# The last three rows of a final RMSNorm, shared out anew between ScalarE, GpSimd and VectorE

## The reference, cut to what matters

```
y = y @ w_out                    # layer 1, the pooling mixer
x = x + gate[:, None, :] * y
return rmsnorm(x, final_g)       # y = x * rsqrt(mean(x*x) + EPS); y * g
```

## Time and profile before

| | |
|---|---|
| median of 3 runs | 1291.89 us (1291.62 to 1292.37) |
| span of the profiled execution | 1290.2 us |
| TensorE busy in it | 1266.2 us, 98% |
| VectorE busy | 985.9 us, 76% |
| ScalarE busy | 642.3 us, 50% |
| GpSimd busy | 315.3 us, 24% |

### The profile page before, as it was taken

How to read it: one execution, slowest core, us unless ns; L and a number is a source line. 1 busy time by engine, 2 the same in 40 slices (tenths; PEclk the granted TensorE clock), 3 DMA queues, 4 the chain that set the end, 5 groups by cost and what they waited for, 6 DMA issues and landing times.

```text
span 1290.2 us, 15455 instructions
## 1 busy us (share of the span) xinstructions
PE 1266.2 (98%) x5639; PEld 1044.3 (81%) x5639; DVE 985.9 (76%) x1155; ACT 642.3 (50%) x904; POOL 315.3 (24%) x182
## 2 busy tenths in 40 slices
PE   5999999999999999999999999999999999999997
PEld 5877888888888888888888888888888888888886
DVE  6889987878878886868467599848748747797677
ACT  7466656465646464635558465234233333443353
POOL 0033443433424343000000013132223121413200
PEclk8999999999999999999999999999999999999999
DMA  9812232323242332597847302232232232882053
GB/s 289 224 49 70 80 121 81 107 83 114 62 122 70 115 106 75 169 382 269 310 155 270 113 17 66 68 97 65 69 95 66 66 98 76 292 285 66 18 177 132
DMA packets 151507, 167.31 MB, mean 130 GB/s; under 512 B 6342, under 2 KB 125318, under 8 KB 151432
## 3 DMA queue, kind: packets, MB, share of 16 engines
q1 hardware_dynamic: 151432, 166.33, 40.0%
HBM read 141.14 MB, written 25.17 MB: 129 GB/s over the span
## 4 chain that ended last, share of the span: by engine, by line
PE 90%; DVE 6%; SPq 1%; issue 1%; ACT 0%; DMA 0%; DVEq 0%; ACTq 0%
PE psum L2382 30%; PE psum L2384 29%; PE psum L2383 29%; DVE whole_x L1985 1%; DVE w_lo L1532 1%; DVE X L1622 1%; SPq L626 1%; PE psum L2529 1%; PE psum L2586 0%; SPq L615 0%; DMA whole_x<-in_mod_w 0%; DVE bufs L1767 0%; DVE w_lo L1554 0%; DVE late L1615 0%; SPq L618 0%
## 5 line engine op out<-in xcount | busy, mean ns | idle before, releaser
L2382 PE MATMUL psum<-X,w_hi 128*128 128x512 f32 x1252 | 489.9, 391 | 1.1 <-DVE X L1666 0.8
L2384 PE MATMUL psum<-X,w_lo 128*128 128x512 f32 x1252 | 488.0, 390 | 0.0
L2383 PE MATMUL psum<-X,w_hi 128*128 128x512 f32 x1252 | 487.9, 390 | 0.0
L2382 PEld LDWEIGHTS psum<-X,w_hi 128*128 128x128 f32 x1252 | 235.5, 188 | 52.2 <-issue 1.7
L2384 PEld LDWEIGHTS psum<-X,w_lo 128*128 128x128 f32 x1252 | 235.4, 188 | 49.4
L2383 PEld LDWEIGHTS psum<-X,w_hi 128*128 128x128 f32 x1252 | 235.5, 188 | 48.6 <-issue 0.2
L984 ACT ACTIVATE w_hi<-ssum 128x512 fp32r<-128x512 f32 x156 | 97.1, 626 | 143.2 <-PE psum L2384 106.8
L1532 DVE TENSOR_TENSOR w_lo<-raw,w_hi 128x1024 fp32r<-128x1024 f32 x82 | 100.9, 1230 | 79.2 <-ACT w_hi L962 78.8
L1554 DVE TENSOR_TENSOR w_lo<-ssum,w_hi 128x512 fp32r<-128x512 f32 x156 | 131.2, 849 | 25.6 <-ACT w_hi L984 25.0
L913 POOL TENSOR_TENSOR ssum<-raw 128x512 f32<-128x512 f32 x39 | 72.8, 1868 | 312.4 <-DMA raw<-in_pool_w_in 253.2
L921 POOL TENSOR_TENSOR ssum<-ssum,raw 128x512 f32<-128x512 f32 x39 | 61.3, 1572 | 340.4 <-DVE w_lo L1554 340.4
(11 more groups left out here) (275 smaller groups left out, 1989.7 us busy)
## 6 DMA issues: line engine op xcount, KB each, us to landing
raw<-in_hy_w_in SPq DMA_DIRECT2D x48, 512.0 KB, 5.1
raw<-in_hy_w_out SPq DMA_DIRECT2D x48, 512.0 KB, 5.1
raw<-in_pool_w_in SPq DMA_DIRECT2D x32, 512.0 KB, 5.0
aux<-in_mod_w SPq DMA_DIRECT2D x16, 512.0 KB, 3.9
y_dram<-bufs SPq DMA_DIRECT2D x16, 512.0 KB, 2.7
raw<-in_mod_w SPq DMA_DIRECT2D x16, 512.0 KB, 5.9
y_dram<-gb_ SPq DMA_DIRECT2D x16, 512.0 KB, 3.4
raw<-in_pool_w_out SPq DMA_DIRECT2D x16, 512.0 KB, 5.9
```

What stands on the lines that cost most here:

```text
L2382: nc.tensor.matmul(out_, whi, xhi, start=first, stop=False, skip_group_check=check)
L2383: nc.tensor.matmul(out_, whi, xlo, start=False, stop=False, skip_group_check=check)
L2384: return nc.tensor.matmul(out_, wlo, xhi, start=False, stop=last, skip_group_check=check)
```

## The change

Rows 5 and 6 are no longer scaled and weighted by one VectorE instruction each. ScalarE scales each of them (`scaled_row`), GpSimd weights row 5 and the first half of row 6 in place, VectorE weights the second half of row 6. For row 7 VectorE multiplies each half by `final` into `PARTS[0]` as soon as its residual is there, and after the reciprocal VectorE scales the first half and ScalarE the second. The reciprocals of rows 5 and 6 move ahead in VectorE's order, and the two halves of row 7's residual are separated. The stores wait for the new semaphores.

```diff
@@ -514,6 +514,10 @@
         out_in = [sem(f"out_in{kp}") for kp in range(KP)]
         out_hi = sem("out_hi")
         out_lo = sem("out_lo")
+        row_scaled = sem("row_scaled")
+        last_final = sem("last_final")
+        half_row = sem("half_row")
+        last_scaled = sem("last_scaled")
         pair_part = sem("pair_part")
         pair_added = sem("pair_added")
 
@@ -741,7 +745,13 @@
                     sp.dma_start(bias1, row).then_inc(bias_in, 16)
 
             def store(b):
-                sp.wait_ge(row_ready, b + 1)
+                if b < 5:
+                    sp.wait_ge(row_ready, b + 1)
+                elif b == 5:
+                    sp.wait_ge(half_row, 1)
+                else:
+                    sp.wait_ge(half_row, 2)
+                    sp.wait_ge(row_ready, 6)
                 sp.dma_start(out[0, b * P:(b + 1) * P, :], XN[1][b]).then_inc(out_done, 16)
 
 
@@ -881,7 +891,10 @@
             for b in range(4, SB - 1):
                 store(b)
             for half, cols in enumerate(HALVES):
-                sp.wait_ge(row_ready, SB + half)
+                if half == 0:
+                    sp.wait_ge(row_ready, 7)
+                else:
+                    sp.wait_ge(last_scaled, 1)
                 sp.dma_start(out[0, (SB - 1) * P:SB * P, cols], XN[1][SB - 1][:, cols]).then_inc(out_done, 16)
             sp.wait_ge(out_done, 16 * (SB + 1))
 
@@ -950,6 +963,12 @@
                                         blocks[:, XOPS["B12"], 1, :], ALU.subtract).then_inc(t13_added, 1)
             for q in range(OUT, len(PAIRS)):
                 sums_of_weights(q)
+
+            pool.wait_ge(gate_in, 32)
+            pool.wait_ge(row_scaled, 1)
+            nc.gpsimd.tensor_tensor(XN[1][5], XN[1][5], final, ALU.mult).then_inc(half_row, 1)
+            pool.wait_ge(row_scaled, 2)
+            nc.gpsimd.tensor_tensor(XN[1][6][:, S1], XN[1][6][:, S1], final[:, S1], ALU.mult).then_inc(half_row, 1)
 
         @block.scalar
         def _(act):
@@ -1499,8 +1518,16 @@
                     step_splits(step)
                 if n in (2, 3, 4, 5):
                     squares(1, n - 2)
-            for b in range(4, SB - 1):
-                squares(1, b)
+            def scaled_row(b):
+
+                act.wait_ge(rstd_ready, SB + b + 1)
+                nc.scalar.activation(XN[1][b], XR[1][b], ACT.Copy, scale=rstd[:, 2, b:b + 1]).then_inc(row_scaled, 1)
+
+            squares(1, 4)
+            squares(1, 5)
+            scaled_row(5)
+            squares(1, 6)
+            scaled_row(6)
 
             b = SB - 1
             for half, cols in enumerate(HALVES):
@@ -1515,6 +1542,10 @@
                 else:
                     nc.scalar.activation(sd[:, 2, b:b + 1], ss[:, 2, b:b + 1], ACT.Sqrt, scale=1.0 / D,
                                          bias=ss[:, 1, b:b + 1]).then_inc(root_done, 1)
+            act.wait_ge(rstd_ready, 2 * SB)
+            act.wait_ge(last_final, 2)
+            nc.scalar.activation(XN[1][b][:, S2], PARTS[0][:, S2], ACT.Copy, scale=rstd[:, 2, b:b + 1])\
+              .then_inc(last_scaled, 1)
 
         @block.vector
         def _(dve):
@@ -2000,14 +2031,24 @@
                 nc.vector.scalar_tensor_tensor(out=XN[1][b], in0=XR[1][b], scalar=rstd[:, 2, b:b + 1], in1=final,
                                                op0=ALU.mult, op1=ALU.mult).then_inc(row_ready, 1)
 
+            def times_final(half):
+
+                b, cols = SB - 1, HALVES[half]
+                dve.wait_ge(o_evac, o_count(1, b, half))
+                nc.vector.tensor_tensor(PARTS[0][:, cols], XR[1][b][:, cols], final[:, cols], ALU.mult)\
+                  .then_inc(last_final, 1)
+
+            def second_half_of_row_6():
+                dve.wait_ge(row_scaled, 2)
+                nc.vector.tensor_tensor(XN[1][6][:, S2], XN[1][6][:, S2], final[:, S2], ALU.mult).then_inc(row_ready, 1)
+
             def last_row_out():
                 b = SB - 1
                 inverse(1, b)
                 dve.wait_ge(rstd_ready, 2 * SB)
-                for cols in HALVES:
-                    nc.vector.scalar_tensor_tensor(out=XN[1][b][:, cols], in0=XR[1][b][:, cols],
-                                                   scalar=rstd[:, 2, b:b + 1], in1=final[:, cols],
-                                                   op0=ALU.mult, op1=ALU.mult).then_inc(row_ready, 1)
+                dve.wait_ge(last_final, 1)
+                nc.vector.tensor_scalar(XN[1][b][:, S1], PARTS[0][:, S1], rstd[:, 2, b:b + 1], None, ALU.mult)\
+                  .then_inc(row_ready, 1)
 
             def modulation_1():
                 dve.wait_ge(*full("mod1"))
@@ -2369,10 +2410,14 @@
             residual(1, 4)
             residual(1, 5)
             row_out(4)
+            inverse(1, 5)
             residual(1, 6)
-            row_out(5)
-            residual(1, 7)
-            row_out(6)
+            residual(1, 7, (0,))
+            inverse(1, 6)
+            times_final(0)
+            residual(1, 7, (1,))
+            times_final(1)
+            second_half_of_row_6()
             last_row_out()
 
         @block.tensor
```

## The result

The changed kernel is slower by 0.21%: its runs have a median of 1295.43 us (21 runs), those of the kernel before, taken with them, 1292.56 us (21 runs); the ratio is 1.0021, 95% interval 1.0015 to 1.0027. Applied to the 1291.89 us from which the prediction started, that is 1294.60 us where 1294.4 was forecast. Of the 1.03 us between 1294.4 and the median of 1295.43, 0.67 is that the kernel before itself came out at 1292.56 in these runs. The same changed kernel, run again later, gave 1.0014, interval 1.0005 to 1.0023 (10 runs).

The account below looks back on a forecast made before the run. TensorE bounds most of the span, then a tail hanging on store 6's issue. Span 1285.80 + 2.48 + 4.40 = 1292.68; adding 2.48 to the 1291.89 median gave 1294.37 us (+0.19%), own range 1294.1 to 1294.6, overall 1293.0 to 1295.4.

Parts of the forecast that it names:

- The burst: Kernel's end: the last megabyte of stores is one DMA burst, ending the span 4.40 us behind store 6's issue.
- Reciprocal of row 5: VectorE's tail: moved ahead of row 6's residual, it starts at 1277.84 and delays that residual by 0.32 us.
- Waits for the two roots: VectorE's tail: its reciprocals of rows 5 and 6 wait 0.24 and 0.30 us for ScalarE's roots.
- GpSimd's row: Tail: GpSimd's weighting of all of row 5, taken as 2.47 us, between 2.28 and 2.57.
- that rival: GpSimd's tail work: a multiply costs more than an addition; 10% more gives 1294.75 us, 30% more 1295.50; chance 0.12.
- First stall: VectorE's second addition of row 6 waits for GpSimd's row 5 and ends 0.55 behind it: 1.63 us.
- The near tie at 1285.25: Tail: VectorE's addition for row 7's second half and GpSimd's half of row 6 ask within 0.02 us; VectorE goes first.
- the first rival: GpSimd is first near 1285.25, ahead of VectorE's addition: store 6 +2.63 us, time 1294.52; chance 0.22.
- Second stall: VectorE's times_final(1), weighting row 7's second half, waits for GpSimd's half of row 6: 1.00 us.
- Store 6: SyncE's store of row 6, which starts the last burst: issued at 1288.28 against 1285.80, +2.48 us.
- The list of what VectorE loses and gains: VectorE's tail: loses two 1.20 us scalings, gains three 0.61 weightings, two root waits and two GpSimd stalls; set against +2.48.
- The rival without exclusion: Tail: GpSimd and VectorE don't block each other on SBUF tensors; store 6 -0.14 us, time 1291.75; chance 0.07.

Follow-up runs that it names:

- the run with one column: Changed kernel with GpSimd's two multiplies cut to one column each, waits and order kept: span ends 7.74 us behind the last matmul, ratio 0.9994.
- the version that did: Against the kernel before: row 5 on ScalarE and GpSimd, products in PSUM, row 6 on VectorE in halves behind row 7's residual; 6.93 us tail, ratio 0.9993, again 0.9987.
- that run: Changed kernel with the gate products of rows 6 and 7 kept in PSUM: span ends 8.19 us behind the last matmul, ratio 0.9998.

## Why the prediction was right

Point by point, shifting my times by the 0.70:

- The burst, +4.40 behind store 6: measured 4.41 (1293.36 - 1288.95). That row 7's shorter work is worth nothing: right, and more than that, with it taken out the span ends 1.21 sooner.
- Reciprocal of row 5 at 1277.84: 1278.54, the same. Waits for the two roots 0.24 and 0.30: 0.24 (1278.54 against 1277.10 + 1.20) and 0.30 (1284.52 against 1283.61 + 0.61). By itself the moved reciprocal costs 0.12, against 0.13 expected.
- GpSimd's row, taken as 2.47 between 2.28 and 2.57: 2.40. The Trainium skill's figure ("GPSIMD Engine Reference", section "Elementwise — side-by-side cycle accounting") had led to an estimate of 2.36, nearer than mine. The multiply costs as much as an addition (1.27 for a half row, undisturbed), so that rival is out.
- First stall 1.63: 2.32 - 0.69 = 1.63. GpSimd's later start (1280.04, expected 1279.97) and its shorter row cancel: that they do is luck, with a row of 2.47 the stall would have been 1.70.
- The near tie at 1285.25: VectorE first, by 0.03 in both executions, so the first rival didn't occur. That was luck as far as the forecast goes: the delay from ScalarE to GpSimd, which decides it, was taken as 0.08 from another pair of engines and came out at 0.14 for row 5 (1278.74 + 1.16 to 1280.04) and 0.07 for row 6 (1284.72 + 1.15 to 1285.94), with a margin of 0.02. Second stall 1.00: 1.64 - 0.69 = 0.95.
- Store 6 +2.48: +2.45. Row 6's second half ends 0.08 sooner than forecast (1288.87, expected 1288.25 + 0.70), and the issue comes 0.08 behind it where 0.03 was taken; so a part of the agreement is two small errors against each other. End of the span behind the last matmul 10.33: 10.31.
- The list of what VectorE loses and gains adds up to 2.60 (-2.40 + 1.83 + 0.54 + 2.63), not to 2.48; it leaves out two reciprocals that are followed by independent work (0.08 instead of 0.19 each) and the dependent start of times_final(1) (0.72 instead of 0.61). The step by step sum has them.
- The rival without exclusion (-0.14): the run with one column comes close to it, store 6 at 3.33 against 3.45 and an end of 7.74 against 7.85.

The time says less than the tail. Applied to 1291.89 the ratio gives 1294.60, the upper edge of my own range of 1294.1 to 1294.6, but its interval reaches from 1293.8 to 1295.4. I gave "within 0.2%" 0.59 and "slower" 0.38, since my sum lay 0.1 us under the mark of 2.58. The tails differ by 2.46, 0.19%; the ratio came out at 1.0021 the first time and 1.0014 the second, and both intervals hold 1.0019 and 1.0020, so the runs do not tell on which side of the mark the change lies. With a sum that close to it the two chances should have stood nearly even.

## What to carry to other kernels

Before giving a part of a busy VectorE's work to GpSimd, look in the timeline for an operation of each that overlap, and see whether both take two tensors from SBUF: if so the work is not shared out but queued, and the wait until GpSimd is done (here 1.63 us for a GpSimd operation of 2.40) is added to VectorE's path. A PSUM operand on VectorE's side lifts the exclusion. That alone didn't make the changed kernel faster than the one before (8.19 against 7.85); the version that did (6.93) changed the order and the stores as well. At the end of a kernel, ask which store's issue starts the last unbroken DMA burst; while the later stores fall inside that burst, work that brings them forward but delays the one that starts it makes the kernel slower.

## What the runs showed of the hardware that was not expected

In the run with one column GpSimd's multiply takes 0.19 us beside a VectorE multiplication that reads PSUM (1279.38), but 0.71 when it asks 0.03 behind an addition with both tensors in SBUF. That is a wait of 0.52, where the half row of the changed kernel waited 0.51 (1.78 - 1.27), so the wait doesn't depend on how little it wants:

```profile
1279.38 0.19 POOL L969 TENSOR_TENSOR whole_x<-whole_x,d_sums 128x1 f32<-128x1 f32 x1 [59.18 <-ACT whole_x L1524]
1283.66 0.71 POOL L971 TENSOR_TENSOR whole_x<-whole_x,d_sums 128x1 f32<-128x1 f32 x1 [4.09 <-ACT whole_x L1524]
```

A product written to PSUM by VectorE and read back costs as much as one in SBUF: the multiplication takes 0.68 to 0.69 and the addition 0.69 in that run, against 0.68 and 0.69 in the earlier trace rows.
